# The order of the work at the start of a turn of the RWKV-7 recurrence

## The reference, cut to what matters

```
S_t = S_{t-1} diag(w_t) - (S_{t-1} kk_t) (a_t*kk_t)^T + v_t k_t^T ;  y_t = S_t r_t
...
y = wkv7_scan(rh, heads(decay), kh, vh, kk, kk * ah)
y = head_group_norm(y, lnx_w, lnx_b)      # mean and variance over the 64 of a head
...
y = (y + bonus) * silu(g)
```

## Time and profile before

| | us |
|---|---|
| median of 3 runs | 2080.65 (2079.68 to 2084.85) |
| profiled execution | 2086.95, span 2085.2 |
| PE busy | 2000.9 (96%) |
| DVE busy | 1395.0 (67%) |
| ACT busy | 1032.0 (49%) |
| POOL busy | 190.1 (9%) |

### The profile page before, as it was taken

How to read it: one execution, slowest core, us unless ns; L and a number is a source line. 1 busy time by engine, 2 the same in 40 slices (tenths; PEclk the granted TensorE clock), 3 DMA queues, 4 the chain that set the end, 5 groups by cost and what they waited for, 6 DMA issues and landing times.

```text
span 2085.2 us, 40330 instructions
## 1 busy us (share of the span) xinstructions
PE 2000.9 (96%) x15310; PEld 1609.8 (77%) x15310; DVE 1395.0 (67%) x2240; ACT 1032.0 (49%) x1829; POOL 190.1 (9%) x214
## 2 busy tenths in 40 slices
PE   5999999988889899999999999999999999999998
PEld 4877777777777776888888888888667778888886
DVE  7788888886566564555554556799777776455455
ACT  6666666666677675333322323442675434233243
POOL 4230000021343222100000000000000000000000
PEclk9999999999999999999999999999999999999999
DMA  4445555562334312233333333333113323333332
GB/s 120 119 142 162 178 185 174 176 155 75 95 84 99 81 56 82 87 96 94 97 101 92 100 91 100 101 91 100 40 43 107 95 61 91 97 95 95 97 93 78
DMA packets 371367, 215.02 MB, mean 103 GB/s; under 512 B 52369, under 2 KB 349737, under 8 KB 371241
## 3 DMA queue, kind: packets, MB, share of 16 engines
q1 hardware_dynamic: 371032, 213.18, 35.1%
q10 hardware_dynamic: 208, 0.06, 0.0%
HBM read 181.68 MB, written 31.52 MB: 102 GB/s over the span
## 4 chain that ended last, share of the span: by engine, by line
PE 88%; ACT 5%; DVE 4%; issue 2%; DMA 1%; SPq 1%; ACTq 0%; DVEq 0%
PE bank L1948 24%; PE bank L1950 23%; PE bank L1949 23%; PE bank L599 2%; PE bank L576 2%; PE bank L613 1%; PE bank L550 1%; PE bank L509 1%; ACT inv L832 1%; PE bank L523 1%; PE bank L588 1%; PE bank L1138 1%; PE bank L542 1%; PE bank L690 1%; PE bank L591 1%
## 5 line engine op out<-in xcount | busy, mean ns | idle before, releaser
L1948 PE MATMUL bank<-xl,w_hi 128*128 128x512 f32 x1568 | 615.6, 393 | 3.5 <-DVE xl L2670 2.5
L1949 PE MATMUL bank<-xl,w_lo 128*128 128x512 f32 x1568 | 611.2, 390 | 0.0
L1950 PE MATMUL bank<-xl,w_hi 128*128 128x512 f32 x1568 | 610.9, 390 | 0.0
L1595 ACT ACTIVATE w_hi<-w_raw 128x1024 fp32r<-128x1024 f32 x278 | 293.1, 1054 | 481.4 <-PE bank L1950 476.9
L2239 DVE TENSOR_TENSOR w_lo<-w_raw,w_hi 128x1024 fp32r<-128x1024 f32 x278 | 342.2, 1231 | 48.7 <-ACT w_hi L1595 40.1
L1948 PEld LDWEIGHTS bank<-xl,w_hi 128*128 128x128 f32 x1568 | 294.5, 188 | 76.6 <-issue 9.9
L1950 PEld LDWEIGHTS bank<-xl,w_hi 128*128 128x128 f32 x1568 | 294.8, 188 | 61.8
L1949 PEld LDWEIGHTS bank<-xl,w_lo 128*128 128x128 f32 x1568 | 294.7, 188 | 60.6 <-issue 0.5
L1948 PE MATMUL bank<-xh,w_hi 128*128 128x512 f32 x448 | 182.8, 408 | 12.2 <-DVE xh L2244 11.9
L1950 PE MATMUL bank<-xh,w_hi 128*128 128x512 f32 x448 | 175.2, 391 | 0.0
L1949 PE MATMUL bank<-xh,w_lo 128*128 128x512 f32 x448 | 175.0, 391 | 0.0
(11 more groups left out here) (385 smaller groups left out, 3084.5 us busy)
## 6 DMA issues: line engine op xcount, KB each, us to landing
w_raw<-in_a_w_in SPq DMA_DIRECT2D x64, 512.0 KB, 4.2
w_raw<-in_b_w_in SPq DMA_DIRECT2D x64, 512.0 KB, 4.1
w_raw<-in_w_ffn_up SPq DMA_DIRECT2D x42, 512.0 KB, 3.9
w_raw<-in_w_in SPq DMA_DIRECT2D x36, 512.0 KB, 3.8
w_raw<-in_a_w_out SPq DMA_DIRECT2D x16, 512.0 KB, 3.8
w_raw<-in_b_w_out SPq DMA_DIRECT2D x16, 512.0 KB, 3.7
w_raw<-in_w_ffn_down SPq DMA_DIRECT2D x16, 512.0 KB, 3.7
d_g<-sq SPq DMA_DIRECT2D x16, 256.0 KB, 2.2
```

Source lines behind the costliest of these rows:

```text
L1595: A(w_hi[0:rows, slot, 0:nkb, 0:ncol], w_raw[0:rows, slot, 0:nkb, 0:ncol], ACT.Copy).then_inc(s_hi, units)
L1948: mm(outp, wh, xlo, start=start, stop=False)
L1949: mm(outp, wl, xhi, start=False, stop=False)
L1950: return mm(outp, wh, xhi, start=False, stop=stop)
```

## The change

The order within the steps 0 to 8 is changed on the three engines. On PE, the transposes of a group stand directly behind its products. Group 0 stays behind the chain's phase of step 0; the groups 1, 2 and 3 stand ahead of the chain's phase of steps 2, 4 and 6. So PE's order is: phase 0 of chunk 0, products 0, transposes 0, phase 1, head norm's sum, products 1, transposes 1, phase 2, phase 0 of chunk 1, head norm's sum, products 2, transposes 2, phase 1, phase 2, head norm's sum, products 3, transposes 3, phase 0 of chunk 2, and so on. On ACT, `turned_out` of group 0 is at step 0, behind the eviction and the y copy, and those of the groups 1, 2 and 3 are ahead of the eviction of steps 2, 4 and 6; `rounded` stays at steps 1, 3, 5 and 7. On DVE, `first_steps` of the groups 1, 2 and 3 stand ahead of the eviction of steps 2, 4 and 6. The head norm stays in its steps. The wait for `s_free` in turn 0 goes into `transposes`. No instruction that computes is added or removed.

```
--- before.py
+++ after.py
@@ -582,6 +582,9 @@
                 a, g = GROUPS[n]
                 if n == 0:
                     pe.wait_ge(R["values_loaded"], LOAD_V * (t + 1))
+                    if t == 0:
+                        pe.wait_ge(s_free[0], U_OUT1 // 2)
+                        pe.wait_ge(s_free[1], U_OUT1 // 2)
                 else:
                     pe.wait_ge(R["products_masked"], 4 * t + n)
                 for c in range(4):
@@ -702,9 +705,9 @@
             pe.wait_ge(s_lfree, CI)
             for t in range(PAIRS + 1):
                 for s in range(3 * NCH):
-                    if t == 0 and s == 1:
-                        pe.wait_ge(s_free[0], U_OUT1 // 2)
-                        pe.wait_ge(s_free[1], U_OUT1 // 2)
+                    if when(t, PAIRS) and s in (2, 4, 6):
+                        products(t, s // 2)
+                        transposes(t, s // 2)
                     if when(t - 1, PAIRS):
                         chain(t - 1, s // 3, s % 3)
                     if t == PAIRS and s in OUT_BLOCKS:
@@ -712,10 +715,11 @@
                     if t == PAIRS and s in (20, 21):
                         x_back_turned(s - 20)
                     if when(t, PAIRS):
-                        if s < 8:
-                            (transposes if s % 2 else products)(t, s // 2)
-                            if t == 0 and s % 2:
-                                fill(4)
+                        if s == 0:
+                            products(t, 0)
+                            transposes(t, 0)
+                        elif s < 8 and s % 2 and t == 0:
+                            fill(4)
                         elif s == S_FIRST:
                             first_inverse(t)
                         elif S_LEVELS <= s < S_LEVELS + 10:
@@ -862,6 +866,8 @@
             for t in range(PAIRS + 2):
                 b, q = t % 2, t - 2
                 for s in range(3 * NCH):
+                    if when(t, PAIRS) and s in (2, 4, 6):
+                        turned_out(t, s // 2)
                     if when(t - 1, PAIRS):
                         recurrence_evac(act, 1, t - 1, s // 3, s % 3)
                     if s == 0 and when(q, PAIRS):
@@ -869,8 +875,9 @@
                     if s == 12 and when(t - 1, PAIRS):
                         y_out(t - 1, 0)
                     if when(t, PAIRS):
-                        if s in (1, 3, 5, 7):
-                            turned_out(t, s // 2)
+                        if s == 0:
+                            turned_out(t, 0)
+                        elif s in (1, 3, 5, 7):
                             rounded(t, s // 2)
                         elif s == 8:
 
@@ -979,6 +986,8 @@
             for t in range(PAIRS + 1):
                 b = t % 2
                 for s in range(3 * NCH):
+                    if when(t, PAIRS) and s in (2, 4, 6):
+                        first_steps(t, s // 2)
                     if when(t - 1, PAIRS):
                         recurrence_evac(dve, 0, t - 1, s // 3, s % 3)
                     if t == 0 and s == 23:
@@ -986,8 +995,8 @@
                     if not when(t, PAIRS):
                         then(s)
                         continue
-                    if s in (0, 2, 4, 6):
-                        first_steps(t, s // 2)
+                    if s == 0:
+                        first_steps(t, 0)
                     elif s in (1, 3, 5, 7):
                         second_steps(t, s // 2)
                     elif s == 8:
```

## The result

The changed kernel takes 2115.48 us (median of 4 runs, 2114.26 to 2118.06) against 2080.58 us of the kernel before in the same comparison: a ratio of 1.0164, 95% interval 1.0149 to 1.0179, 34.9 us slower. The forecast was 2111 us in a range of 2095 to 2126.

The account below looks back on a forecast made before the run. The prediction took PE, nearly full in strict alternation with the chain (18.05 of 19.3 us), as the bound. Six turns at +4.96 us and turn 1 at +0.8 gave +30.6, from 2080.65 to 2111 us, range 2095 to 2126.

Parts of the forecast that it names:

- The walk: Steps 0 to 8, first L523 to chunk 3's, timed piece by piece: 24.29 us against 19.33, +4.96 a turn.
- The seven waits: PE idle before chain phases and norm sums in the reordered part of turns 2 to 7: 6.48 us against 1.25.
- the 18.0 that was named as a sign: Expected PE busy time, in us, within the 24.3 us from first L523 to chunk 3's, turns 2 to 7.
- Where the loss is from: Transposes 1 to 3 leave gaps where the chain waits; ACT's 1.3 us `turned_out` precedes an uncovered eviction: +4.96 us a turn.
- Turn 1: Reordered part without head norm: 20.7 us where it was 19.85, +0.8 us, as no norm sum waits for ACT.
- The clock: PE's granted clock in the reordered parts stays at 1.00 despite 6.5 of 24.3 us idle: no cost.
- a rival at 7%: The clock falls in each of six turns, 2.8 us each, +16.8 us on top, time 2128; chance 7%.
- the prediction's own signs: Wrong if turns 2 to 7's reordered windows stay near 19 us, the later part shrinks, or their clock is below 1.00.
- The rest of the turns: Later part of each turn, 26.7 us in turn 3, keeps its order and is shifted whole: 0 us.
- a later part that shrinks: Sign of being wrong: the turn after chunk 3's L523 gets shorter, where it was forecast as long as before.
- The sum: All turns together: 6 x 4.96 + 0.8 = +30.6 us, median from 2080.65 to 2111 us; chance 80%.

Follow-up runs that it names:

- e1: The kernel before with only PE's order changed as in the changed kernel, ACT and DVE as before: 2117.13 us, ratio 1.0139.
- e2: The changed kernel, but in steps 2, 4 and 6 ACT and DVE evict before `turned_out` and `first_steps`: 2132.18 us, ratio 1.0215.
- e3: The changed kernel with products and transposes paired behind the chain's phases of steps 0, 2, 4, 6, evictions first: 2128.71 us, ratio 1.0201.
- e6: The kernel before with the new order for group 1 alone, in turns 1 to 7: 2100.22 us, ratio 1.0064.
- e9: The changed kernel with the head norm moved in turns 2 to 7 (PE sums at steps 2, 4, 6, 9; ACT's work later): 2092.31 us, ratio 1.0034.
- e8: The changed kernel itself, run again beside the others on the same chip: 2119.07 us, ratio 1.0159 to the kernel before.
- e7: The changed kernel with 4, 6 and 4 unused 128x64 matmuls behind the chain's phases of steps 2, 4, 6: 2113.58 us, ratio 1.0131.
- e4: The changed kernel with 8, 12 and 6 unused 128x64 matmuls behind the chain's phases of steps 2, 4, 6: 2119.28 us, ratio 1.0149.

## Why the prediction was right, point by point

- *The walk.* L523 of chunk 1 at 8.25: measured 8.31. L523 of chunk 2 at 19.12: measured 19.12 to 19.19 in turns without a fall of the clock. L523 of chunk 3 at 24.29: 24.07 to 24.12 in such turns. The seven waits were placed and released as forecast: 1.28, 0.47, 1.67, 0.78, 1.02, 0.95 and 0.31 us forecast, 1.03, 0.26, 1.29, 0.69, 0.69, 0.74 and 0.27 measured. Each is shorter than forecast, and PE's busy time in the part is 19.1 us, not the 18.0 that was named as a sign: the pieces that stand beside a wait are longer in the rows than the forecast took them from start to start (a norm sum 1.12 us for 0.95, phase 1 0.45 for 0.33). The starts, which set the time, are hardly touched by it. The same kind of walk gave e1, e2, e3 and e6 within 0.35 us of the turns at full clock.
- *Where the loss is from.* Forecast as cover moved and ACT's copies ahead of an eviction. That the pairing on PE costs is shown by e1, e3 and e6; ACT's copies ahead of the eviction are not a cost by themselves, since e2, without them, is slower. The prediction gave the norm sums 2.2 of its 6.5 us of waits. What it did not say, and e9 shows, is how much more hangs on the head norm: with the norm in the bare gaps the same order costs 1 us a turn, not 4.7.
- *Turn 1*: +0.8 forecast, -0.1 measured. PE's 4.43 us of idle time there are 4.60 over the whole stretch (the window of the earlier trace rows ends 0.15 us before L523), and 4.80 in the changed kernel: the bare handoffs took the place of other waits. It fits the last point, but it is no rule that a turn without norm sums loses nothing: e1 loses 2.5 us in turn 1 and e6 0.4.
- *The clock*: kept at 1.00 in the forecast, with its fall as a rival at 7% and 2.8 us a turn. It did fall, in five of six turns in the first profile and three of six in e8, at 0.8 to 1.6 us each (e7 against e8: 5.5 us). This term was put at nothing and measured about 7 us in the first profile, and by the prediction's own signs (a clock below 1.00 in these windows) this part of it was wrong; the rival's 2.8 us a turn was too much. What brings the fall on stays open. PE's idle time in the part does not tell it: e1's parts, idle for 5.3 of 24.5 us, are all at 1.00, and the changed kernel's, idle for 5.0, are not. Nor is it the stretch of 575 to 577 alone: turn 7 has the same waits at 1.00; in turn 5 the clock fell only at 686.5, at L696 behind waits of 0.69 and 0.74 us; and turn 1 of the kernel before has waits of 0.82 and 1.08 us with 0.7 us of work between them, and kept 1.00. The warning of the Trainium skill (TensorE: Matmul & The Clock Gate, "A second HAM failure mode: psum-queue depth-cycling") tells of it for bf16 matmuls of 512 columns; the trace of turn 3, with f32 matmuls, agrees: the granted clock goes to 0.50 after idle stretches of 1.29 and 0.69 us, and is back by 581 us.
- *The rest of the turns* unchanged: as far as can be seen. They sum to 7.7 us less in the profile (a later part that shrinks was one of the signs of being wrong), mostly since the execution of before had rests of 29.4 us in turns 2 and 5 and this one had none. Such rests appear in other runs, too (29.6 in turn 2 of e7, 29.7 in e8), so they are not the change's. What brings them on was not tried. The medians differ by 34.9 us and the parts alone by 35.4, which leaves nothing for the rests to give back.
- *The sum*: +30.6 forecast. From the parts, 6 x 4.75 - 0.1 = 28.4, and 7.0 for the clock, gives the 35.4 of the profiles, against 34.9 of the medians. So the order by itself cost 2 us less than forecast and the clock 7 more. The mechanism of the sum is right; that the total came within 4.3 us, and well inside the range, owes something to errors of opposite sign.

## What to carry to other kernels

Where a dependent chain and independent work share an engine, the independent pieces are worth what they cover: two pieces in one gap leave another gap bare. Here the first such pair cost 2.0 us a turn and three cost 4.7, and most of it came back when another piece was put into the bare gaps. Making the other engine serve the chain first does not help if a piece ahead on the shared engine waits for that engine, too (e2, e3). Before such a reordering, write the order of the one engine down and ask of every pair of neighbours on the chain what lies between them; small pieces whose inputs are ready by then (here a norm sum of 0.95 us) belong there. And idle stretches of TensorE can have a second price in its clock, in some executions and not in others.

## What the runs showed of the hardware

- In turn 3 the granted clock fell to 0.50 after PE had been without a matmul from about 574.7 to 576.0 and from 576.7 to 577.4, and was back at 1.00 at 581. The same program shows the fall in a turn in one execution and not in another; with 14 unused small matmuls a turn it did not come in any of these parts of the profiled execution, and the program was 5.5 us faster.
- Halving the columns of a small f32 matmul saved nothing. The 8 unused matmuls of 128x64 in e4 (16 records, two a matmul) take 1.93 us up to the next start, 0.24 each. The 4 of 128x128 that `fill` issues in turn 0 of the kernel before (8 records) start 0.11 us apart from record to record, and so do those of e4: 0.22 us a matmul in both. The rows, of e4 and of the kernel before:

```profile
571.28 2.00 PE L716 MATMUL bank<-mean_d,ident 128*128 128x64 f32 x16
573.21 0.45 PE L523 MATMUL bank<-sv,st_q 128*64 128x64 f32 x8
```

```profile
432.76 1.06 PE L699 MATMUL bank<-mean_d,ident 128*128 128x128 f32 x8
```
